# Expert outputs stored by slot and gathered at the end, and experts taken in an order that depends on their pairs: a two-layer diffusion step on one core

## The reference

```python
g_sel = argmax(xt @ w_rg + b_rg)                  # one of 4 groups
top_v, top_i = top_k(e_logits[g_sel], 2)          # 2 of its 8 experts
gates = softmax(top_v) * p_g
# per expert e: y[token] += gate * ((silu(x @ w_gate[e]) * (x @ w_up[e])) @ w_down[e])
```

## Time and profile before

| what | value |
|---|---|
| median of 3 runs | 1420.31 us (1420.12 to 1421.23) |
| the profiled execution's own time | 1422.74 us |
| its span | 1420.6 us |
| mean granted clock of TensorE in it | 0.898 |
| busy: PE, PEld, DVE, ACT, POOL | 76%, 40%, 28%, 13%, 18% |
| DMA moved | 389.73 MB, mean 274 GB/s |
| chain that ended last | DMA 42%, PE 31%, issue 11%, DVE 10% |
| of it: weights w_down and w_up | 21% and 10% |
| of it: DMA ybuf<-yo, DMA xg<-xmod | 5%, 3% |

### The profile page before, as it was taken

The page is one execution under the profiler, slowest core; times in us unless marked ns, Lnnn a source line. Parts: engine busy times, 40 slices in busy tenths (PEclk is TensorE's granted clock), DMA queues, the critical chain, the costliest instruction groups (busy, mean ns, idle before and its releaser), DMA issues.

```text
span 1420.6 us, 26863 instructions
## 1 busy us (share of the span) xinstructions
PE 1083.1 (76%) x9857; PEld 565.1 (40%) x9858; DVE 401.5 (28%) x955; ACT 180.4 (13%) x485; POOL 254.3 (18%) x450
## 2 busy tenths in 40 slices
PE   5899998797677777657557999899838557778781
PEld 1333345444344444323223444565434323444440
DVE  0120217768311111101034002565861001111117
ACT  0110026300000000000012000552000000000000
POOL 2000002201133333212112010000023212333330
PEclk9999998898699999878787999899859977999996
DMA  9866891117979999999975993201089999989922
GB/s 370 302 241 257 338 363 68 60 36 269 415 283 387 414 414 413 413 415 416 411 266 119 119 149 116 74 1 60 36 328 413 412 415 416 413 347 372 414 109 109
DMA packets 85411, 389.73 MB, mean 274 GB/s; under 512 B 17612, under 2 KB 18124, under 8 KB 57720
## 3 DMA queue, kind: packets, MB, share of 16 engines
q1 hardware_dynamic: 63136, 349.77, 63.6%
q0 software_dynamic: 15200, 36.74, 9.1%
q10 hardware_dynamic: 7032, 2.68, 0.7%
HBM read 379.66 MB, written 17.44 MB: 280 GB/s over the span
## 4 chain that ended last, share of the span: by engine, by line
DMA 42%; PE 31%; issue 11%; DVE 10%; ACT 2%; DVEq 1%; POOLq 1%; POOL 1%; SPq 1%; ACTq 0%; PEldq 0%
DMA ring<-in_w_down_dram 21%; PE ps L806 15%; DMA ring<-in_w_up_dram 10%; DMA ybuf<-yo,idy 5%; PE ps L967 3%; PE ps L1065 3%; DMA xg<-xmod,idx 3%; PE ps L1083 2%; DMA ring<-in_w_ada_dram 1%; PE ps L782 1%; PE ps L912 1%; PE ps L894 1%; PE ps L901 1%; PE ps L934 1%; POOLq L451 1%
## 5 line engine op out<-in xcount | busy, mean ns | idle before, releaser
L1065 PE MATMUL ps<-ring,xs 128*32 128x256 f32 x4928 | 315.3, 410 | 120.2 <-DMA ring<-in_w_up_dram 80.7
L1065 PEld LDWEIGHTS ps<-ring,xs 128*32 128x32 f32 x4928 | 186.2, 117 | 244.0 <-issue 166.9
L806 PE MATMUL ps<-ring,hT 128*128 128x512 f32 x576 | 255.0, 602 | 8.1 <-ACT hT L630 4.3
L1083 PE MATMUL ps<-ring,hm 128*32 128x256 f32 x2464 | 157.8, 397 | 31.0 <-ACT hm L740 26.8
L806 PEld LDWEIGHTS ps<-ring,hT 128*128 128x128 f32 x576 | 109.6, 192 | 152.6 <-issue 142.3
L1083 PEld LDWEIGHTS ps<-ring,hm 128*32 128x32 f32 x2464 | 73.5, 113 | 91.0 <-ACT hm L740 41.1
L1540 DVE COPY yo<-ps 128x256 f32<-128x256 f32 x73 | 31.0, 425 | 229.2 <-DMA ybuf<-yo,idy 171.0
L541 POOL DMA_INDIRECT xg<-xmod,idx x77 | 80.8, 1050 | 66.0 <-POOL idx L538 62.2
L1532 DVE TENSOR_TENSOR hp<-sg,ps 128x128 f32<-128x128 f32 x73 | 21.0, 288 | 252.6 <-ACT sg L737 232.3
L737 ACT ACTIVATE sg<-ps 128x128 f32<-128x128 f32 x73 | 20.2, 277 | 561.2 <-PE ps L1065 554.9
L967 PE MATMUL ps<-ring,qT 128*128 128x512 f32 x192 | 85.7, 607 | 2.0 <-DVE qT L1348 1.6
(11 more groups left out here) (264 smaller groups left out, 833.9 us busy)
## 6 DMA issues: line engine op xcount, KB each, us to landing
ring<-in_w_gate_dram SPq DMA_DIRECT2D x82, 1024.0 KB
ring<-in_w_up_dram SPq DMA_DIRECT2D x82, 1024.0 KB
ring<-in_w_down_dram SPq DMA_DIRECT2D x82, 1024.0 KB
ring<-in_w_ada_dram SPq DMA_DIRECT2D x48, 1024.0 KB, 8.2
ring<-in_w_qkv_a_dram SPq DMA_DIRECT2D x12, 1024.0 KB, 5.3
ring<-in_w_qkv_b_dram SPq DMA_DIRECT2D x12, 1024.0 KB, 16.1
modb<-mdram POOLq DMA_DIRECT2D x12, 512.0 KB, 6.8
qkv<-ybuf SPq DMA_DIRECT2D x6, 1024.0 KB, 8.5
```

Of the source, the lines that this page charges most:

```text
L806: ins = mm(ps[:, 2 * t + hf, :], lhs[:, k, t * P:(t + 1) * P], raw[:, slot, kk * D + hf * 512:kk * D + (hf + 1) * 512], start=(k == 0), st ...
L1065: ins = mm(ps[j * BLK:(j + 1) * BLK, 1, 0:W].rearrange("p (a n) -> p a n", a=2), xs[:, k, :], w[:, :, at:at + FW], start=(k == 0), stop=(k ...
L1083: ins = mm(ps[j * BLK:(j + 1) * BLK, 5, 0:WD], hm[:, 2 * c + q, :], ring[:, slot + GU + c, q * D + j * WD:q * D + (j + 1) * WD], start=(c ...
```

## The change

Four things. (1) The store of a block is no longer an indirect DMA on POOL but a plain one issued by ACT behind its own two steps of the block. It writes all 32 rows of the block, used or not, to rows 32 b to 32 b + 31 of `ybuf`. `rowi`, `idy` and their steps on DVE and POOL go. (2) At the end of the experts POOL gathers from `ybuf` by `sloti`: six indirect DMAs, each of 128 rows of 4 KB, in place of SP's three plain loads, after waits for all stores and all weight loads. (3) `ybuf` has 1920 rows now, and since unused slots may hold anything, one DMA of SP writes zeros over it in layer 0, between w_o and the last conditioning wave; POOL sets the row of zeros. (4) The key of an expert is its number less 385/8192 (0.047) per pair: six small matmuls are added to the two at L1022 and L1023. The two picks stay first.

In blocks per expert the order becomes:
- layer 0 before: 3, 4, 2, 1, 1, 2, 4, 2, 2, 2, 1, 1, 2, 1, 1, 1, 2, 1, 1, 1, 1, 1; after: 3, 4, 2, 1, 4, 1, 2, 2, 2, 2, 1, 1, 2, 1, 1, 2, 1, 1, 1, 1, 1, 1 (expert 8 from the seventh place to the fifth)
- layer 1 before: 2, 2, 1, 1, 1, 1, 1, 1, 3, 1, 6, 2, 1, 4, 1, 1, 1, 5, 1; after: 2, 2, 1, 1, 1, 1, 1, 6, 3, 1, 4, 1, 2, 5, 1, 1, 1, 1, 1 (expert 21 from the eleventh place to the eighth, 25 from the fourteenth to the eleventh, 30 from the eighteenth to the fourteenth)

```diff
...
 NBX = NB + 2
+YROWS = -(-NBX * BLK // P) * P
...
 WO_N = 4
+EARLIER = 385.0 / 8192.0
...
         sloti = sb("sloti", [P, 2 * NT], I32)
-        rowi = sb("rowi", [P, NBX], I32)
-        idy = sb("idy", [P, 1], I32)
         toki = sb("toki", [P, NBX], I32)
+        early = sb("early", [P, NE])
...
-        ybuf = nc.dram_tensor("ybuf", (TOPK * NT * P + BLK, D), F32).ap()
+        ybuf = nc.dram_tensor("ybuf", (YROWS, D), F32).ap()
...
         gu_used, dn_used = sem2("gu_used"), sem2("dn_used")
-        idx_rdy, idy_rdy, gath = sem2("idx_rdy"), sem2("idy_rdy"), sem2("gath")
+        idx_rdy, gath = sem2("idx_rdy"), sem2("gath")
+        zero_rdy, y_zero = sem("zero_rdy"), sem("y_zero")
...
                 if l == 0:
+                    sp.wait_ge(zero_rdy, 1)
+                    sp.dma_start(ybuf.rearrange("(p a) (h d) -> p (a h) d", p=P, d=512),
+                                 zrow[:, :].unsqueeze(1).to_broadcast([P, 2 * YROWS // P, 512])).then_inc(y_zero, 16)
...
                 n_load = table(sp, T_NLD, BUFS + 1, NE)
-                n_blk = table(sp, T_NBLK, 24, NB)
...
-                wait_apart(sp, sp_steps, y_wr[l], n_blk * 16)
-                for t in range(NT):
-                    sp.dma_start(ypair[:, 2 * t:2 * t + 2, :],
-                                 ybuf[0:2 * NT * P, :].rearrange("(s t p) d -> p t s d", s=TOPK, p=P)[:, t])\
-                        .then_inc(yg_ld[l][t], 16)
...
+            pool.memset(zrow[:, :], 0.0).then_inc(zero_rdy, 1)
...
-                def store(b):
-
-                    wait_apart(pool, pool_steps, yo_rdy[l], b + 2)
-                    pool.tensor_copy(idy[:, :], rowi[:, bass.ds(b, 1)] if not isinstance(b, int) else rowi[:, b:b + 1])\
-                        .then_inc(idy_rdy[l], 1)
-                    wait_apart(pool, pool_steps, idy_rdy[l], b + 1)
-                    pool.indirect_dma_start(out=ybuf.rearrange("r (j w) -> (r j) w", j=G),
-                                            out_offset=bass.IndirectOffsetOnAxis(ap=idy[:, 0:1], axis=0),
-                                            in_=yo[:, :], in_offset=None,
-                                            bounds_check=G * (TOPK * NT * P + 1) - 1, oob_is_err=False).then_inc(y_wr[l], 16)
-
...
                 next_gather(1)
-                store(0)
...
                     next_gather(b + 1)
-                    store(b)
...
                 wait_apart(pool, pool_steps, y_wr[l], n_blk * 16)
+                n_load = table(pool, T_NLD, BUFS + 1, NE)
+                for s in range(RING):
+                    wait_apart(pool, pool_steps, moe_land[l][s], n_load * 16)
+                for t in range(NT):
+                    for k in range(TOPK):
+                        at = TOPK * t + k
+                        pool.indirect_dma_start(out=ypair[:, at, :], out_offset=None, in_=ybuf,
+                                                in_offset=bass.IndirectOffsetOnAxis(ap=sloti[:, at:at + 1], axis=0),
+                                                bounds_check=YROWS - 1, oob_is_err=False)\
+                            .then_inc(yg_ld[l][t], 16)
...
                 n_blk = table(act, T_NBLK, 24, NB)
+                if l == 0:
+                    act.wait_ge(y_zero, 16)
...
+                    act.wait_ge(yo_rdy[l], b + 2)
+                    dst = ybuf.rearrange("(b t) (j w) -> b j t w", t=BLK, j=G)[bass.ds(b, 1) if not isinstance(b, int) else slice(b, b + 1)]
+                    act.dma_start(dst.rearrange("o j t w -> (o j) t w"), yo[:, :]).then_inc(y_wr[l], 16)
+
...
                 for t in range(NT):
-                    act.wait_ge(yg_ld[l][t], 16)
+                    act.wait_ge(yg_ld[l][t], 16 * TOPK)
...
                 pe.wait_ge(key_rdy[l], 1)
-                mm(ps[0:NE, 3, P:P + NE], ones[0:1, 0:NE], rt[0:1, 1400:1400 + NE], start=True, stop=True)
-                mm(ps[0:NE, 3, P + NE:P + NE + 1], rt[0:1, 1400:1400 + NE], ones[0:1, 0:1], start=True, stop=True)\
-                    .then_inc(key_ps[l], 1)
+                mm(ps[0:NE, 3, P:P + NE], ones[0:1, 0:NE], rt[0:1, 1400:1400 + NE], start=True, stop=False)
+                for t in range(NT):
+                    mm(ps[0:NE, 3, P:P + NE], early[:, :], a_all[:, t, :], start=False, stop=(t == NT - 1))
+                mm(ps[0:NE, 3, P + NE:P + NE + 1], rt[0:1, 1400:1400 + NE], ones[0:1, 0:1], start=True, stop=False)
+                for t in range(NT):
+                    ins = mm(ps[0:NE, 3, P + NE:P + NE + 1], a_all[:, t, :], early[:, 0:1], start=False, stop=(t == NT - 1))
+                ins.then_inc(key_ps[l], 1)
...
+            v.memset(early[:, :], -EARLIER)
...
                     v.tensor_scalar(rowf.rearrange("p (t k) -> p t k", k=TOPK)[:, :, k], cst[:, C_TOK:C_TOK + NT],
-                                    1.0 + k * NT * P, None, ALU.add)
+                                    1.0, None, ALU.add)
...
                 dve.wait_ge(rt_pe[l], 5)
-                val, empty, half, tok = (rt[:, 3600 + i * NBX:3600 + (i + 1) * NBX] for i in range(4))
+                val, empty, tok = (rt[:, 3600 + i * NBX:3600 + (i + 1) * NBX] for i in range(3))
...
-                v.tensor_scalar(empty, val, 0.0, None, ALU.is_lt)
-                chain(v.tensor_scalar(half, val, float(NT * P), -float(NT * P), ALU.is_ge, ALU.mult))
-                chain(v.tensor_tensor(tok, val, half, ALU.add))
-                chain(v.scalar_tensor_tensor(tok, empty, cst[:, C_SKIP:C_SKIP + 1], tok, ALU.mult, ALU.add))
+                chain(v.tensor_scalar(empty, val, 0.0, None, ALU.is_lt))
+                chain(v.scalar_tensor_tensor(tok, empty, cst[:, C_SKIP:C_SKIP + 1], val, ALU.mult, ALU.add))
...
                 v.tensor_scalar(toki[:, :], tok, cst[:, C_PIECE:C_PIECE + 1], None, ALU.add).then_inc(tok_rdy[l], 1)
-                chain(v.scalar_tensor_tensor(half, empty, cst[:, C_SPARE:C_SPARE + 1], val, ALU.mult, ALU.add))
-                v.tensor_scalar(rowi[:, :], half, float(G), cst[:, C_PIECE:C_PIECE + 1], ALU.mult, ALU.add)
-
...
```

More of the change, by code:

```diff
@@ L176, in backbone_kernel @@
         (btab,) = overlay([("btab", [P, HEADS * BM * GRID_W], F32)])
-        yo, xs, xg, sg, hp, hm, _, mst, mbias = overlay([
+        yo, xs, xg, sg, hp, hm, _, mst, mbias, zrow = overlay([
             ("yo", [P, WD], F32), ("xs", [P, KD, BLK], F32), ("xg", [P, WD], F32),
@@ L180, in backbone_kernel @@
             ("small_gap", [P, 3136 - (WD + KD * BLK + WD + 3 * FW)], F32), ("mst", [P, 2, 512], F32),
-            ("mbias", [G, 2, 512], F32)])
+            ("mbias", [G, 2, 512], F32), ("zrow", [P, 512], F32)])
         sb("small_region", [P, 6144])
```

## The result

| | median | range | ratio, 95% interval |
|---|---|---|---|
| before (4 runs beside it) | 1420.69 us | 1420.12 to 1421.23 | |
| after (4 runs) | 1578.75 us | 1575.94 to 1581.39 | 1.1112 [1.1086, 1.1138] |

The change costs 158 us where 12 were forecast. The profiled execution after took 1576.4 us, its span is 1574.6 us. From its page: span; packets by queue; the chain that ended last by engine and by line; groups of instructions; DMA issues (count, KB each, us to landing).

The account below looks back on a forecast made before the run. Weights bound layer 0; in layer 1 block pace, set by the store's wait at 8.1 us, sets the end. Layer 0 +5.3 and layer 1 +6.8 made +12.1, so 1432 us; range 1410 to 1446.

Parts of the forecast that it names:

- What bounds it: Experts' stages: weights bound layer 0 and layer 1 until 1182.28 us, then block pace (PE, store or gather chain), 7.42 us average.
- The store's path: Plain ACT store under weight traffic: copy 0.44 + 0.2 + 4.0 + 3.0 + 0.5 = 8.1 us a block, against 7.55.
- Both bounds, 6.3 and 9.0: Limits in us of the store's sum per block, with its packets taking 1.2 us or 3.8 us.
- The rule that was weighed: An engine drains some 9 to 17 descriptors before switching queue, so a store goes in one turn; sum then 1423 us.
- The ends of the layers: From last copy to `ypair`: 7.8 us after, against 11.5 in layer 0 and 8.9 in layer 1; gain 3.7 and 1.1.
- Zeros: SP's 7.9 MB of zeros, 19 us at 414 GB/s, hidden in idle DMA time during layer 0's attention: cost 0.
- routing: Six matmuls added, two DVE steps gone: net +0.8 us before the first gather, passed on in layer 0, hidden in layer 1.
- bytes: Stores now write unused rows too, delaying weight traffic: 3.7 us in layer 0, 1.5 us in layer 1.
- Order: New expert order: layer 0 stall of 4.5 us (2.0 at the old pace); layer 1 saving given back as idle DMA.
- faster: Rival, chance 0.22: short store and gather below 5.3 us, so PE bounds at pace 7.05; sum -10.1, 1410 us.
- even: Rival, chance 0.2: plain store takes no longer than now, gather sets the pace, p = 7.5; 1423.6 us.
- slower by more: Rival, chance 0.13: packets take 3.8 us or wait for a gather's too; store chain 9.0, p = 8.4; 1450 us.

Follow-up runs that it names:

- e1_flat: The changed kernel with the store's destination walked as 128 pieces in a line, still one plain ACT DMA (output rows mixed): 1458.97 us, 1.0251 of before.
- e8_gather: The kernel before with six indirect POOL gathers in place of SP's three plain loads at the end of a layer: 1425.41 us, 1.0026 of before.
- e2_four: The changed kernel with its store cut into four plain ACT DMAs of 32 partitions, same result: 1445.55 us, 1.0175 of before.
- e9_four_old: The changed kernel with its store as four plain DMAs of 32 partitions and the old order of experts: 1442.61 us, 1.014 of before.

## Why the prediction was wrong

- **What bounds it: right.** The copy to `yo` hung on the store's wait, the weights' stream and PE were where they were said to be. That "behind ACT's new wait nothing is late" was wrong: the Silu at 1211.72 came 7.2 us after its gate and up. In the block shown this lay beside the store; what it costs by itself was not measured.
- **The store's path: the step that failed.** The forecast had ACT's queue with 73 x 128 packets of 1 KB, and that is what ran. It gave them "nine turns" of 16 engines, 3.0 us; they ran in 33 turns of 4 engines, 10.8 us. Every other term of that sum held: 4.0 us to the first packet (3.9 measured), 0.5 from the last to the copy (0.5), 0.33 us a turn (0.33). With 33 turns the same sum is 0.44 + 0.2 + 4.0 + 11.0 + 0.5 = 16.1 us against 15.78 measured; with nine it is 8.1, and e1_flat, which really has nine, measured 7.52. Both bounds, 6.3 and 9.0, assumed 16 engines, so the range could not hold the result.
- **The clue was in the earlier trace rows.** The stores at 363.77 us write four rows of 2 KB each (8 KB to a row of `mdram` cut by G = 4), two of them: 8 packets of data among 16. The other 8 are then the closing packets, 4 each: a store whose slowest size is 4 ran on 4 engines in the trace of before. The load of 22.4 to 26.2 us, which gave the upper bound, had 128 rows. I counted its packets and not its engines. The Trainium skill, page "DMA: Bandwidth & Descriptors", section "Why a DMA increments its semaphore by 16 and not by 1", says that the number of engines is the largest up to 16 that divides the slowest size of both sides. The 132, 144 and 192 packets of a block (4, 16 and four times 16 closing ones) agree with it.
- **The rule that was weighed.** The section "Queues, rings and completion order" of the same page of the Trainium skill has an engine drain several descriptors in a turn. In the 10.9 us above an engine of the four ran 33 packets of the store and, as a share of the 779, some 49 of the weights; by that page's figure (an estimate) the 32 rows would have been through in two to four turns. The counts speak against it here, as rows 7 did.
- **The ends of the layers: wrong in sign.** Forecast -3.7 and -1.1, measured +2.8 and +3.6. The chain of after has the terms, layer 1 first:

```profile
1528.03 3.27 DMA ybuf<-yo
...
1533.76 0.35 POOL qkv L569
...
1535.07 5.12 DMA qkv<-ybuf,sloti
```

```profile
793.33 6.07 DMA ybuf<-yo
...
801.50 0.35 POOL qkv L569
...
802.85 5.35 DMA qkv<-ybuf,sloti
```

In layer 1: store 3.27 (2.4 taken; 1.71 in e1_flat with 16 engines), from its landing to the first gather 2.46 (0.8), to the second 1.31 (1.05), its landing 5.12 (3.4). The waits, the table and the start of POOL's issue were put at 0.8 us in all. And the second gather, 0.5 MB behind another 0.5 MB, needs 5.12 us from its issue, where the plain load of the same 1 MB needs 5.08: the 1.31 us between the two issues come on top. e8_gather has the same end of layer 1 with the old store, so there it is the gathers. In layer 0 e8_gather shows only +0.8; in the kernel after the last store of layer 0 itself took 6.07 us. The two loads that POOL issues "earlier, since no store holds it" now move 1 MB ahead of and beside it, and its first packet comes later than 4 us after the issue (1.2 in layer 1): what was counted as a gain went into the store.
- **Zeros and routing: right; bytes: somewhat high.** Forecast +5.2 for the bytes, +3.1 [1.3, 5.0] measured. The 7.9 MB of zeros took 35.2 us to land, and the first weights of layer 0 are issued at 347.7 us, 348.3 before. Routing shows between these weights and the first gather: 370.48 - 348.25 = 22.2 us before, 370.55 - 347.61 = 22.9 after, +0.7 where 0.8 was forecast.
- **Order: not settled.** +4.5 forecast for layer 0 at 8.1 us a block (2.0 at the old pace); by the table, one execution each, +2.2 at 8.35 and -0.5 at the old pace. Layer 1, forecast at 0, has -3.6 and -1.5 in single executions, which the medians of e2_four and e9_four_old don't bear out. It stays open.
- **The sum, had the engines been right.** e2_four comes nearest to it: layer 0 +8.9 to its last copy (0.8 + 3.7 + 4.5 = 9.0 forecast), layer 1 +6.8 (7.9 forecast), the ends +7.2 (-4.8 forecast); +23.3 us by the medians. So the ends, 12.0 us off, are a second term that failed: alone they double the forecast's +12. That layer 0 fits so well is in part luck: e2_four issues four DMAs, not one. The DMA that was costed, one on 16 engines, is e1_flat's, and in layer 0, where its experts, blocks and order are those of the kernel after, it costs +2.6 to the last copy (375.4 against 372.8), not 9.0. A kernel with that DMA and the right rows was not run. Of the rivals, faster is out; even and slower by more are too, as after stands, and no rival held 4 engines.

## What to carry to other kernels

Before a plain DMA is costed, write down both access patterns after folding and look at the slowest size of each: a column block of a wider buffer, `(j t) w` with j = 4, is a DMA on 4 engines. The count of packets in a trace shows it: for one DMA, what is over the rows of data is the number of engines. A price from a row of the trace holds only for a transfer with as many engines; and a step that leaves a queue for another should be timed with all the waits and tables at its new place.

## What the runs showed of the hardware that was not expected

- The number of engines matters far more beside other traffic. The store of after on 4 engines landed in 3.27 us with no weights moving (1528.03, above) and in 13 to 15 us among them. On 16 engines (e1_flat) it landed in 1.71 us with no weights moving, and the next copy came 6.9 us after the issue among them:

```profile
1413.47 1.71 DMA ybuf<-yo
```

- On 4 engines the first packet came 1.2 us after the issue with no weights moving, 3.9 us in the stream.
- On an engine with a full weights' queue a store's packet of 1 KB waited some 0.33 us for its turn, at 4 and at 16 engines alike, in the stores shown: the delay is packets per engine times the turn. At 2 engines the turn was 0.26.
- A slow store limits itself: once the ring is full, the stream stops, and the store is quick again. So twice the interval in traffic (15.78 against 7.53 us) gave 1.11 in time, not more.
- TensorE's granted clock fell with the gaps, from 0.93 to 0.72 in 1182 to 1244 us. The down of a block took 3.48 us at 1197.42, with 0.54 granted (near the level of 1.2 GHz), and 1.93 at 790.65, with 1.00 (2.4 GHz); it lay beside the store and cost nothing here.
